# Hybrid decoder trunk on one core: state outputs, score mask and value products in another order

## What is computed

```python
proj = hn @ w_in
u, q, k, v, g = jnp.split(proj, [S5_WIDTH, S5_WIDTH + RET_WIDTH, ...], axis=-1)
y_s5 = s5_mixer(u, lam_re, ...)      # B u, complex scan over time, Re(C x) + D u, gelu, gate
q, k = apply_rope(q), apply_rope(k)  # six heads of 256
inner = jnp.einsum('bhid,bhjd->bhij', qc, kc) * dmask      # in retention(), chunks of 128
o = jnp.einsum('bhij,bhjd->bhid', inner, vc) + ...
y_ret = jax.nn.silu(g) * norm(o)
return jnp.concatenate([y_s5, y_ret], axis=-1) @ w_out
```

## Time and profile before

| | |
|---|---|
| median of three runs | 2188.27 us (2188.1 to 2195.16) |
| profiled execution | 2189.09 us, its span 2187.3 us |
| TensorE busy | 2150.4 us, 98% of the span |
| VectorE busy | 1486.7 us, 68% |
| ScalarE busy | 1036.7 us, 47% |
| GpSimd busy | 657.6 us, 30% |
| granted TensorE clock, mean | 0.996 of full speed |

### The profile page before, as it was taken

How to read it: one execution, slowest core, us unless ns; L and a number is a source line. 1 busy time by engine, 2 the same in 40 slices (tenths; PEclk the granted TensorE clock), 3 DMA queues, 4 the chain that set the end, 5 groups by cost and what they waited for, 6 DMA issues and landing times.

```text
span 2187.3 us, 47247 instructions
## 1 busy us (share of the span) xinstructions
PE 2150.4 (98%) x18506; PEld 2125.3 (97%) x18506; DVE 1486.7 (68%) x1777; ACT 1036.7 (47%) x1354; POOL 657.6 (30%) x608
## 2 busy tenths in 40 slices
PE   8999999999999999999999999999999999999997
PEld 8988999999999999999999999999999999999997
DVE  6799995777666555666666666677666555666665
ACT  5555554445444444445444455445444444445443
POOL 5665550133434003343211000133434003343311
PEclk9999999999999999999999999999999999999998
DMA  6444444555554565555456433554544555455453
GB/s 256 174 157 143 156 159 170 180 193 189 198 191 171 190 212 207 193 194 194 161 186 226 154 118 133 185 192 183 211 174 180 192 203 212 183 201 188 170 197 117
DMA packets 66144, 398.78 MB, mean 182 GB/s; under 512 B 9216, under 2 KB 11264, under 8 KB 30592
## 3 DMA queue, kind: packets, MB, share of 16 engines
q1 hardware_dynamic: 60192, 391.15, 50.1%
q10 hardware_dynamic: 5856, 6.27, 0.9%
HBM read 395.29 MB, written 2.10 MB: 182 GB/s over the span
## 4 chain that ended last, share of the span: by engine, by line
PE 89%; DVE 5%; issue 2%; DVEq 1%; ACT 1%; DMA 0%; POOL 0%; POOLq 0%; ACTq 0%
PE PS L1539 27%; PE PS L1540 27%; PE PS L1543 27%; DVE lo L774 3%; PE PS L1534 1%; PE PS L1536 1%; PE PS L1535 1%; DVEq L989 1%; DVE S L1005 0%; PE PS L1664 0%; PE PS L1905 0%; PE PS L1906 0%; PE PS L1921 0%; PE PS L1698 0%; ACT hi L369 0%
## 5 line engine op out<-in xcount | busy, mean ns | idle before, releaser
L774 DVE TENSOR_TENSOR lo<-raw,hi 128x1024 fp32r<-128x1024 f32 (+2 forms) x826 | 981.2, 1207 | 490.3 <-ACT hi L369 485.5
L369 ACT ACTIVATE hi<-raw 128x1024 fp32r<-128x1024 f32 (+2 forms) x826 | 787.0, 970 | 727.6 <-PE PS L1543 688.4
L1539 PE MATMUL PS<-XS,hi 128*128 128x256 f32 x3584 | 844.9, 278 | 8.5 <-ACT hi L369 8.5
L1540 PE MATMUL PS<-XS,hi 128*128 128x256 f32 x3584 | 839.6, 277 | 0.0
L1539 PEld LDWEIGHTS PS<-XS,hi 128*128 128x128 f32 x3584 | 674.8, 188 | 11.9 <-issue 11.5
L1540 PEld LDWEIGHTS PS<-XS,hi 128*128 128x128 f32 x3584 | 674.7, 188 | 0.4
L1543 PE MATMUL PS<-XS,lo 128*128 128x256 f32 x3584 | 481.6, 277 | 0.0
L1543 PEld LDWEIGHTS PS<-XS,lo 128*128 128x128 f32 x3584 | 441.9, 188 | 0.0
L1539 PE MATMUL PS<-YF,hi 128*128 128x256 f32 x1408 | 331.8, 276 | 0.0
L1540 PE MATMUL PS<-YF,hi 128*128 128x256 f32 x1408 | 331.8, 276 | 0.0
L1496 POOL TENSOR_TENSOR ctmp<-apad,cws 128x512 f32<-128x512 f32 x88 | 132.0, 1521 | 525.9 <-DVE apad L823 525.9
(11 more groups left out here) (264 smaller groups left out, 2373.8 us busy)
## 6 DMA issues: line engine op xcount, KB each, us to landing
raw<-in_ffn_up SPq DMA_DIRECT2D x176, 1024.0 KB, 4.8
raw<-in_ffn_dn SPq DMA_DIRECT2D x128, 704.0 KB, 4.1
raw<-in_w_in SPq DMA_DIRECT2D x51, 1024.0 KB, 4.8
raw<-in_w_oe SPq DMA_DIRECT2D x16, 1024.0 KB, 4.9
raw<-in_w_oo SPq DMA_DIRECT2D x16, 1024.0 KB, 4.8
raw<-in_mla_dn SPq DMA_DIRECT2D x9, 1024.0 KB, 4.8
raw<-in_w_ukv SPq DMA_DIRECT2D x8, 1024.0 KB, 4.8
raw<-in_w_uq SPq DMA_DIRECT2D x8, 768.0 KB, 4.2
```

The lines of the kernel that those rows point to most:

```text
L369: act.activation(hi[:, p % SLOTS, 0:n], raw[:, u % SLOTS, off:off + n], ACT.Copy).then_inc(hi_ready, 1)
L774: V.tensor_tensor(lo[:, p % SLOTS, 0:n], raw[:, u % SLOTS, off:off + n], f(hi[:, p % SLOTS, 0:n]), ALU.subtract).then_inc(lo_ready, 1)
L1539: mm(PS[:, bank, 0:T], wh, x[:, 0:T], start=first, stop=False)
L1540: mm(PS[:, bank, 0:T], wh, x[:, T:2 * T], start=False, stop=False)
```

## The change

Three edits. On TensorE the value step runs each piece's 16 products with the high weights first, behind a wait for `hi` alone, and the 8 with the low weights after them; `c_x(0)` and `b_u(2)` follow its third piece instead of the second. On VectorE the mask stands ahead of the fourth gate split, and `scan(1)` follows the third key split of the next head instead of the second. On ScalarE `bu_copy(2)` and `bu_copy(3)` follow the third gate piece instead of the second.

```diff
@@ scalar, even_head
                 for i in range(4):
                     split(p0 + 12 + i, 16, r)
-                    if s5 and i == 1:
+                    if s5 and i == 2:
                         bu_copy(2)
                         bu_copy(3)
@@ vector, even_head
-                splits(p0 + 12, 16, r)
+                splits(p0 + 12, 16, r, ("std",) * 3)
                 dve.wait_ge(s_done, H_(1, 1))
                 dve.wait_ge(dec_in, H_(16, 16))
                 V.tensor_tensor(Pm[:, 0:T], PS[:, 4, 0:T], dec[:, :], ALU.mult)
                 V.tensor_tensor(Pm[:, T:T + P], PS[:, 4, T:T + P], dec[:, 0:P], ALU.mult).then_inc(pm_ready, 1)
+                split(p0 + 15, 16, r)
                 if glu:
                     dve.wait_ge(glu_sig, 1)
                     V.tensor_tensor(sigs, sigs, U[:, :, :], ALU.mult).then_inc(glu_mul, 1)

                 for i in range(4):
                     split(p0 + 16 + i, 16, r)
-                    if s5 and i == 1:
+                    if s5 and i == 2:
                         scan(1)
@@ tensor, even_head
                 for i in range(4):
                     p = p0 + 8 + i
+                    pe.wait_ge(hi_ready, at(p + 1, 16, r))
+                    for tt in range(2):
+                        for k in range(4):
+                            kk = 4 * i + k
+                            for o in (0, T):
+                                mm(PS[:, b + tt, 0:T], XS[:, kk, o + tt * P:o + (tt + 1) * P], hi[:, p % SLOTS, k * T:(k + 1) * T],
+                                   start=kk == 0 and o == 0, stop=False)
                     piece(p, 16, r)
                     for tt in range(2):
                         for k in range(4):
                             kk = 4 * i + k
-                            xh = XS[:, kk, tt * P:(tt + 1) * P]
-                            xl = XS[:, kk, T + tt * P:T + (tt + 1) * P]
-                            wh, wl = hi[:, p % SLOTS, k * T:(k + 1) * T], lo[:, p % SLOTS, k * T:(k + 1) * T]
-                            mm(PS[:, b + tt, 0:T], xh, wh, start=kk == 0, stop=False)
-                            mm(PS[:, b + tt, 0:T], xh, wl, start=False, stop=False)
-                            ins = mm(PS[:, b + tt, 0:T], xl, wh, start=False, stop=kk == KD - 1)
+                            ins = mm(PS[:, b + tt, 0:T], XS[:, kk, tt * P:(tt + 1) * P], lo[:, p % SLOTS, k * T:(k + 1) * T],
+                                     start=False, stop=kk == KD - 1)
                     ins.then_inc(piece_done, 1)
-                    if s5 and i == 1:
+                    if s5 and i == 2:
                         c_x(0)
                         b_u(2)
```

## The result

The changed kernel takes 2193.44 us in the median of 20 runs (2190.08 to 2199.49), the kernel before 2188.47 (2186.86 to 2195.72). The ratio is 1.0019, with a 95% interval of 1.0013 to 1.0025. Forecast was a gain of 2.5 us; measured is a loss of about 4 to 5.

The account below looks back on a forecast made before the run. TensorE, busy 98% of the span, was taken as the bound, so only its waits (11.9 us) could be won. Gains 0.6, 2.0 + 0.5 and 3.9, together 7.0, less 4.5 gave 2.5: 2188.27 to 2185.8, range 2180.5 to 2190.5.

Parts of the forecast that it names:

- step 5: VectorE, scan(1) after the next head's third key split: b_u(0) waits 1.5 us in heads 2 to 4, losing 4.5.
- Step 1: TensorE, state outputs and b_u(2) one piece later: 0.2 us won in each of heads 2 to 4, 0.6 together.
- Step 2: TensorE, value products with high parts first: gains of 2.0 us in head 0 and 0.5 in head 1.
- Step 3: ScalarE's copies after G2's high part: GpSimd's rotation starts 2.7 us later, covered because scan(1) starts near 203.
- Step 4: VectorE, mask ahead of the fourth gate split: the wait for masked scores goes whole, 3.9 us over heads 2 to 4.
- dear end: At b_u(0), the longest wait priced, 1.9 us: scan(1) takes 5.80 beside GpSimd's phasor products, the split behind it 1.7.
- Rival (b): b_u(0) of heads 2 to 4: scan(1) late enough to eat all gains; at 3.3 us per head, 2191.2; chance 0.12.
- rival (c): After the heads: slow matmul rhythm, +3.5 us, 2189.3, or 2214 if stuck for a third of the run; chance 0.08.
- The rival that the change does not move anything: TensorE's waits merely change names, 2188.3 us; chance 0.10.

Follow-up runs that it names:

- fill_all: Changed kernel plus unread matmuls: 24 before V2's low products in head 1, 14 before b_u(0) in heads 2 to 4; 2190.28 us, ratio 0.9999.
- scan_back: Changed kernel with scan(1) alone put back behind the second key split; 2182.21 us, ratio 0.9971.
- scan_fill: Kernel before with scan(1) behind the third key split and 14 unread matmuls before b_u(0) in heads 2 to 4; 2195.1 us, ratio 1.0027.
- cx_back: Changed kernel with c_x(0), b_u(2) and their copies back behind the second piece; 2195.17 us, ratio 1.0027.
- the version that takes the gains: Kernel before with mask ahead of fourth gate split, high parts first, c_x(0) and b_u(2) between V2's high and low products; 2180.74 us, ratio 0.9965.
- scan_only: Kernel before with scan(1) alone moved behind the third key split; 2198.05 us, ratio 1.0043.

## Why the prediction was wrong

**Direction and range.** It said 2185.8, faster, within 2180.5 to 2190.5; it is 2193.4, slower. Two steps failed: step 5's wait was priced too low (4.5, measured 5.9), and the half clock behind long waits was put at nothing, without a reason (3 to 5 us).

**What bounds the kernel** held: the answer was a matter of waits on TensorE. But the harm was priced from lengths of waits alone, and here idle time on TensorE had a second price that no list of waits shows.

**Step 1** (state outputs later, 0.6): V2 waits 1.0 for its low part as written, but nothing is won in heads 2 to 4: from V0 to the score products they take 15.52, 15.49 and 15.54, before 15.40, 15.57 and 15.54. **Step 2**: head 0 gained 1.88 of 2.0. Head 1 was to gain 0.5 by making one wait of 3.3 out of two; the wait came (3.15 in the view), and then half clock for 1.67, so it lost 1.4. Without the half clock it would have won 0.3. This is the first failed step: the text had the number 3.3 and the names of both old waits, and asked nothing about the clock behind it. **Step 3** held: copies and rotation late by about 2.7 (the rotation's copy at 190.40), covered. **Step 4**: forecast 3.9, measured 4.2; the mask was ready 4.6 to 4.8 us before TensorE took it. (G2's split was not slowed to 2.8 or more as forecast: the three gate splits of head 2 took 3.49 together. It was GpSimd's first copy beside the third of them that took longer, 1.20 where it took 0.19 before.)

**Step 5** had the right place and mechanism and too small a size. The wait at `b_u(0)` was put at 1.5, between 0.5 and 1.9; it measured 2.07, 1.98 and 1.86, at and just over the dear end. The term is 5.9 and not 4.5. The row that it was to be nearest to, the scan beside GpSimd's ladder of products, was the whole answer: 2.87, 1.22, 1.76 and a split of 1.75 in the trace after, against 2.89, 1.77 and 1.7 read from before. There was no reason to go below it. Nor are the two ends taken alike: e + 9.3 against e + 8.96 is a wait of 0.34, where 0.5 stands, and e + 10.8 one of 1.84. The prediction named the Trainium skill, page "SBUF — State Buffer", section "SBUF: two separate sides", for the dear end: a VectorE operation with two SBUF inputs and a GpSimd operation take turns at a shared port pair. The trace agrees, with 1.76 for the scan's last product and 1.75 for the split, beside GpSimd's products, where both took 1.2 without them.

**Sum.** With the measured sizes and without the clock: 0 + 1.9 + 0.3 + 4.2 - 5.9 = 0.5, so zero for practical purposes, as fill_all shows (0.9999). Half clock then adds 3 us in the median (fill_all against the changed kernel) and up to 5 (scan_back's surplus over the waits, of which 1.8 lie in the attention layer in the profiles). So some 2 us of the miss are waits and 3 to 5 the clock. None of the rivals had the clock. Rival (b), slower, named the right place, but by a longer wait, which did not come; rival (c), the slow rhythm, exists and costs its 3.5 (3.4 in scan_fill's profile), but the other eleven profiles, before and after among them, have the projection at 113 ns. The rival that the change does not move anything is closest in the waits alone.

**Why 2193.4 and not 2190.6.** The mean clock of the 20 runs of the changed kernel goes from 0.995 to 0.993; nine at 0.995 have a mean span of 2190.2, nine at 0.994 2192.2, two at 0.993 2195.6. So eleven of the twenty executions have a lower mean clock than the profiled one, and so more half clock; but at 0.995 alone the spans go from 2188.3 to 2194.0, so the clock is not all of it. Which waits drop the clock differs from one execution to the next: cx_back's profile has it behind heads 1, 2 and 4, the changed kernel's behind 1 and 2 with the same waits.

**Open.** Spans of one kernel at one mean clock still differ by some 3.5 us (the version that takes the gains: 2176.8 and 2176.9 against 2180.3 and 2180.5, all at 0.996). So do fill_all's two groups. The projection's slow rhythm has that size and was seen in one profile; that it explains the difference everywhere is argued, not shown. What sets the rhythm is open too, and so is what decides the half clock in the attention layer.

## What to carry to other kernels

Price an operation moved in an engine's queue by what it is then anchored to: scan(1), behind one more split, waited for a high part that waits for TensorE, and so for the very engine that it was to feed. Be wary of joining two short waits of TensorE into one long one: here that brought half clock. Where a wait must stay, shorten it by products that need nothing, or fill it. A change with several edits is worth trying edit by edit: here the mask alone won 4.1, and one misplaced line cost 11.

## What the runs showed of the hardware

Waits of 1.8 to 2.0 us on TensorE inside the heads, with dense matmuls around them, were followed by a granted clock of 0.5 for some 3.4 us in some places and not in others: the changed kernel's profile has it behind one of three (2.00), scan_only's behind two of three (1.99 and 1.80, not 1.82). Waits of 1.0 to 1.7 us in the heads had none behind them in any of the twelve profiles; those of 3.15 to 3.6 always had, once for 10.2 us. One stretch of 3.4 us in a head cost 1.56 to 1.67 us. Matmuls that nobody reads, put into the wait, went with a clock of 1.00 in the heads and were worth 3 us net in two kernels (2193.44 to 2190.28, 2198.05 to 2195.1). Full-clock matmuls of 256 columns ran at 113 or 118 ns from start to start, for a whole step or a whole projection (91 against 87 records in 10 us), with the same instructions.
